# Hybrid decoder layer on one core: a square moved ahead, two pipeline points one step later, and a weight load inside a DRAM exchange

## The reference

```
p = rms_norm(h_res, norm_mix_g) @ w_in
xc, b_gate, c_gate = split(p[..., :3072], 3)
y_conv = b_gate * conv3(c_gate * xc, conv_w)
z = p + (prev_token(p) - p) * mu          # token shift of r, k, v and the low-rank parts
kk = k * k_k ; kk = kk / max(norm_per_head(kk), 1e-12)
S_t = S_{t-1} * w_t + (S_{t-1} @ a_t) b_t^T + v_t k_t^T ;  y_t = S_t @ r_t
y = layer_norm_per_head(y) * lnx_w + lnx_b + sum(r * k * r_k) * v ;  y = y * g
h_res += concat(y_conv, y) @ w_out
h_res += relu(rms_norm(h_res) @ w_up)^2 @ w_down ;  out = rms_norm(h_res)
```

## Time and profile before

| | |
|---|---|
| median of 3 runs | 2480.15 us (2478.11 to 2480.57) |
| the profiled execution's own time | 2474.11 us |
| its span | 2472.4 us |
| PE busy | 2421.4 us (98%) |
| DVE busy | 1128.8 us (46%) |
| ACT busy | 784.8 us (32%) |
| the eight pairs | about 112 to 868 us of the span |

### The profile page before, as it was taken

One profiled execution on the slowest core, in us unless ns is written; L12 is line 12 of the kernel. 1 busy time (PEld: TensorE's weight loads), 2 busy tenths in 40 slices (PEclk: granted clock), 3 DMA queues, 4 the chain that ended last, 5 costly groups with the idle time before them and its releaser, 6 DMA issues.

```text
span 2472.4 us, 41991 instructions
## 1 busy us (share of the span) xinstructions
PE 2421.4 (98%) x16510; PEld 2046.5 (83%) x16510; DVE 1128.8 (46%) x1725; ACT 784.8 (32%) x1320; POOL 184.8 (7%) x224
## 2 busy tenths in 40 slices
PE   6999999999999999999999999999999999999997
PEld 6989989989989778788888888888888888888886
DVE  6367567576576654533333333333233333333343
ACT  6434343334334322332232232222222221322233
POOL 4001001011010132000000000000000000000032
PEclk8999999999999999999999999999999999999999
DMA  8333343342442643323233333233233333332332
GB/s 209 90 91 79 94 97 80 87 101 73 97 97 78 176 138 90 89 86 108 81 107 98 86 102 94 84 104 94 86 104 94 93 101 87 87 110 81 98 94 94
DMA packets 506892, 243.65 MB, mean 99 GB/s; under 512 B 102992, under 2 KB 500688, under 8 KB 506192
## 3 DMA queue, kind: packets, MB, share of 16 engines
q1 hardware_dynamic: 500512, 222.70, 33.3%
q0 software_dynamic: 6208, 18.37, 2.3%
HBM read 224.08 MB, written 16.92 MB: 97 GB/s over the span
## 4 chain that ended last, share of the span: by engine, by line
PE 88%; DVE 4%; DMA 4%; ACT 2%; issue 1%; SPq 1%; ACTq 0%; DVEq 0%
PE PD L1349 64%; PE PD L1352 17%; PE PD L1540 1%; DMA w_raw<-in_w_in 1%; DMA gram<-NA 1%; DMA inverse<-UU 1%; DVE w_lo L948 1%; DMA UU<-gram 1%; PE PW L1503 1%; DMA x_rows<-in_x 0%; DVE act_lo L953 0%; PE PW L1405 0%; DVE uni L1112 0%; PE PW L1467 0%; PE PW L1382 0%
## 5 line engine op out<-in xcount | busy, mean ns | idle before, releaser
L948 DVE TENSOR_TENSOR w_lo<-w_raw,w_hi 128x512 fp32r<-128x512 f32 x780 | 543.9, 731 | 308.2 <-ACT w_hi L684 305.0
L684 ACT CAST w_hi<-w_raw 128x512 fp32r<-128x512 f32 x780 | 456.7, 620 | 705.8 <-PE PD L1349 518.4
L1349 PE MATMUL PD<-act_lo,w_hi 128*128 128x512 f32 x1344 | 531.3, 395 | 0.0
L1349 PE MATMUL PD<-act_hi,w_hi 128*128 128x512 f32 x1344 | 529.2, 394 | 1.5 <-DVE res L1225 1.5
L1349 PE MATMUL PD<-act_hi,w_lo 128*128 128x512 f32 x1344 | 528.5, 393 | 0.0
L1349 PE MATMUL PD<-u_hi,w_hi 128*128 128x512 f32 x1024 | 409.7, 400 | 0.0
L1349 PE MATMUL PD<-u_hi,w_lo 128*128 128x512 f32 x1024 | 403.4, 394 | 0.0
L1349 PE MATMUL PD<-u_lo,w_hi 128*128 128x512 f32 x1024 | 401.5, 392 | 0.0
L1352 PE MATMUL PD<-act_hi,w_hi 128*128 128x264 f32 x1376 | 297.9, 298 | 10.0 <-DVE act_lo L953 9.9
L1349 PEld LDWEIGHTS PD<-act_hi,w_hi 128*128 128x128 f32 x1344 | 252.5, 188 | 63.4 <-DVE w_lo L948 1.9
L1349 PEld LDWEIGHTS PD<-act_lo,w_hi 128*128 128x128 f32 x1344 | 252.0, 188 | 58.2 <-issue 0.2
(11 more groups left out here) (278 smaller groups left out, 1571.8 us busy)
## 6 DMA issues: line engine op xcount, KB each, us to landing
w_raw<-in_w_up SPq DMA_DIRECT2D x256, 256.0 KB, 3.3
w_raw<-in_w_down SPq DMA_DIRECT2D x256, 256.0 KB, 3.1
w_raw<-in_w_in SPq DMA_DIRECT2D x200, 256.0 KB, 3.3
w_raw<-in_w_out SPq DMA_DIRECT2D x64, 256.0 KB, 2.8
x_rows<-in_x SPq DMA_DIRECT2D x4, 1024.0 KB, 8.0
residual<-res POOLq DMA_DIRECT2D x2, 2048.0 KB, 11.9
out<-rows SPq DMA_DIRECT2D x8, 512.0 KB, 4.9
uni<-inverse SPq DMA_DIRECT2D x16, 240.0 KB, 4.2
```

The source lines that it names most:

```text
L684: nc.scalar.copy(w_hi[:, q % RING], w_raw[:, q % RAW]).then_inc(hi_split, 1)
L948: V.tensor_tensor(w_lo[:, q % RING], w_raw[:, q % RAW], w_hi[:, q % RING].bitcast(F32), ALU.subtract).then_inc(lo_split, 1)
L1349: ins = M(pd_seq(n), w, v[:, k, first:first + SEQ], start=begin, stop=end)
```

## The change

The table changes five numbers: `tr` and `amv` each get one dense step more ahead of them, `ahead4` and `ahead5` one less. Running sums before: tr 28, gram1, base1 and base2 31, amv 33, ahead3 45, ahead4 50, ahead5 54. After: tr 29, gram1, base1 and base2 32, amv 35, ahead3 47, ahead4 51, ahead5 54. From x16 on nothing in the table moves. The square of the keys of pair j+1 is issued by ScalarE in the last name of pair j, ahead of the copies of the value tile, with a semaphore of its own. The read half of the second exchange moves from load 17 to load 18.

```diff
@@ -68,13 +68,13 @@
 
 
 
-PACE = dict(ss=2, low=5, vtr=5, ahead0=6, gram0=8, tr=2, gram1=3, base1=0, base2=0, amv=2, ahead1=4, ahead2=4,
-            ahead3=4, ahead4=5, ahead5=4, x16=3, t16=2, x32=2, tt32=2, pq=2, gh=3, y0=5, z2=4, z3=2, z4=1, z5=2, z6=1,
+PACE = dict(ss=2, low=5, vtr=5, ahead0=6, gram0=8, tr=3, gram1=3, base1=0, base2=0, amv=3, ahead1=4, ahead2=4,
+            ahead3=4, ahead4=4, ahead5=3, x16=3, t16=2, x32=2, tt32=2, pq=2, gh=3, y0=5, z2=4, z3=2, z4=1, z5=2, z6=1,
             z7=2, z8=2, y=2, var=3, ahead6=4)
 
 PE_STEPS = [n for n in PACE if n[:4] != "base" and n[:5] != "ahead"]
 Z_STEPS = ("z2", "z3", "z4", "z5", "z6", "z7", "z8")
-ACT_STEPS = ["sq", "nrm", "for_sig", "sigw", "siga", "for_exp", "vtok", "epv", "em", "ep", "gs", "ghi", "btok",
+ACT_STEPS = ["nrm", "for_sig", "sigw", "siga", "for_exp", "vtok", "epv", "em", "ep", "gs", "ghi", "btok",
              "ktok", "bonb", "atok", "mv", "t16", "tt32", "warm", "pq", "sqc", "yk", "std"]
 DVE_STEPS = (["kk", "ssm", "inv", "ld", "scan", "mid", "mu", "epv", "gs", "kkn", "tfac", "kp",
               "at", "b", "bt", "rt", "kt", "rb", "gram0", "bon", "glo", "gram1", "diag"]
@@ -317,7 +317,7 @@
     low_done, low_sig, low_top = sem("low_done"), sem("low_sig"), sem("low_top")
     gram_out, gram_back = sem("gram_out"), sem("gram_back")
     inv_out, inv_back, inv_cleared = sem("inv_out"), sem("inv_back"), sem("inv_cleared")
-    z_done = sem("z_done")
+    z_done, k_squared = sem("z_done"), sem("k_squared")
     conv_step = sem("conv_step")
     conv_stored, y_stored = sem("conv_stored"), sem("y_stored")
     zeroed = sem("zeroed")
@@ -443,6 +443,7 @@
                 dve("ut")
                 for m in range(2):
                     sp.dma_start(inv_blocks[:, m], UU[0:NBLK, 1 - m, :].rearrange("b (s t) -> b s t", t=BASE)).then_inc(inv_out, 16)
+            if i == 18:
                 sp.wait_ge(inv_out, at(32, 32, j))
                 for a in range(2):
                     r = slice(a * C, (a + 1) * C)
@@ -708,6 +709,10 @@
             nc.scalar.copy(halves(shifted[0:rows_, 1:T + 1]), pd(n)[0:rows_])
             nc.scalar.activation(halves(keep[0:rows_, :]), pd(n)[0:rows_], ACT.Copy, scale=mun).then_inc(evacuated[n % 2], 1)
 
+        def square_keys(j):
+            act.wait_ge(z_done, at(5, 3, j))
+            nc.scalar.activation(fsq, zk[:], ACT.Square, scale=p_("k_k", j)).then_inc(k_squared, 1)
+
 
         act.wait_ge(zeroed, 2)
         act.wait_ge(par_loaded, N_PAR)
@@ -718,6 +723,8 @@
             if n == 5:
                 for q in range(Q_PAIR + EDGE_LEAD, Q_PAIR + LEAD):
                     split(q)
+            if n == 5:
+                square_keys(0)
             take_shifted(n, 4 * (n + 1), mun[0:rows_], z_before=n if n else None, rows_=rows_)
             for q in range(4 * n + 8, 4 * n + 12):
                 if q < Q_PAIR + EDGE_LEAD:
@@ -762,7 +769,6 @@
 
             def steps_of(name):
                 if name == "ss":
-                    done("sq", nc.scalar.activation(fsq, zk[:], ACT.Square, scale=feat("k_k")))
                     dve("ssm")
                     done("nrm", nc.scalar.activation(fsq, fsq, ACT.Sqrt))
                     done("for_sig", nc.scalar.activation(warm[:], eps_t[:, 0:1], ACT.Sigmoid))
@@ -813,6 +819,8 @@
                 if name == "var":
                     pe("var")
                     done("std", nc.scalar.activation(ysq, PW[:, 0, :], ACT.Sqrt, bias=eps_t[:, 1:2]))
+                if name == "ahead6" and not last:
+                    square_keys(j + 1)
 
             splits, tiles, y_split = 0, 0, 0
             for name, k in zip(PACE, schedule()):
@@ -1377,7 +1385,7 @@
 
             def steps_of(name):
                 if name == "ss":
-                    act("sq")
+                    pe.wait_ge(k_squared, j + 1)
                     for a in range(2):
                         ins = M(PW[:, 2 + a, 0:HALF], same_head[:], half(fsq, a), start=True, stop=True)
                 if name == "low":
```

## The result

The changed kernel takes 2487.96 us (median of 6 runs, 2486.32 to 2490.15), the kernel before on the same chip 2478.0 us (2474.04 to 2480.57). The ratio is 1.004, 95% interval 1.0027 to 1.0053: slower by about 10 us, which is more than the measurement's uncertainty. The forecast was 2493.7 us, in a range of 2476 to 2506. Against the profiled executions' own times (2474.11 and 2487.06 us) the change costs 12.95 us; the sum said 13.6. The profiled execution of the kernel before is one of its quickest, 3.9 us under the median of the six, and the changed kernel's lies 0.9 us under its own.

The account below looks back on a forecast made before the run. The prediction took TensorE's own matmuls as the bound, with about 12 us of waits. Its terms, -5.4 + 16.8 - 1.0 + 3.2 = +13.6 us, gave 2487.7 us, plus 6.0 to the median: 2493.7 us, range 2476 to 2506.

Parts of the forecast that it names:

- the sum: Whole kernel: -5.4 + 16.8 - 1.0 + 3.2 = +13.6 us against the profiled execution's 2474.1 us.
- The inversion is later: On VectorE: inversion starts 4.00 us later (0.60 + 3.40), less earlier DMA waits of 3.5 us over the pairs.
- A new wait at x16: TensorE at x16, first seven pairs: waits 1.5 to 2.5 us for the reads of the inverted blocks.
- t16: TensorE at t16: 2.80 us later in pairs 0 to 4, 2.23 in 5 and 6; +16.8 us together.
- The square: At the start of each pair: TensorE's wait for the square goes in all eight, -5.4 us, between 0 and 6.
- Contention of the gate's store: The store of `cx` falls beside the reads and load 18: 0.45 us in seven pairs, +3.2 us.
- The clock: Rival: clock falls to half level behind new waits in seven pairs, +11.9 us, 2505.6 us; chance 0.12.
- The last pair: Inversion only 2.2 us later, t16 0.2 us earlier, part of L1540's 1.8 us wait goes: -1.0 us.
- The late landing of the write: Second exchange: write up to 1.8 us later per pair, unsummed; as rival +6.4 us, 2500.1 us, chance 0.08.
- load 18 landed: Rival: load 18 quicker by 2 us or more, so x16 alone sets t16; 2479 us, no change; chance 0.15.
- "faster" rival: Way from `ut` to x16 has over 4 us of slack, all waits go: -13.4 us, 2466.8 us; chance 0.15.

Follow-up runs that it names:

- e1: The changed kernel with VectorE's split of quarter 13 and the convolution put back behind the inversion: 2457.99 us, ratio 0.9925 to the kernel before.
- e5: The kernel before with only the new numbers of the table, square and load 17 as before: 2502.76 us, ratio 1.0113.
- e6: The kernel before with quarter 13's split and the convolution ahead of the inversion on VectorE, quarter 13's rounding ahead of ScalarE's AMV copies: 2501.06 us, ratio 1.0096.
- e2: The kernel before with only the square of the keys issued ahead of the value tile's copies: 2468.93 us, ratio 0.997.
- e3: The kernel before with only load 17 moved between the write and the reads of the second exchange: 2469.67 us, ratio 0.9973.
- e9: The changed kernel with the table of before, so only the square ahead and load 17 between write and reads: 2460.35 us, ratio 0.9927 to the kernel before.
- e10: e1 run once more on the same chip as e9: 2459.52 us, ratio 0.9928 to the kernel before.
- e4: The kernel before with only VectorE's split of quarter 13 and the convolution put ahead of the inversion: 2531.38 us, ratio 1.0223.
- e7: The kernel before with the new numbers of the table and the convolution held behind the inversion: 2479.76 us, ratio 1.0013.

## Why the prediction was right

The direction and the mechanism held: five VectorE instructions ahead of the inversion, a chain through DRAM that passes the delay on, and a new wait at x16. The forecast of +13.6 us stands against 12.9 between the traces and 10.0 between the medians. The forecast time of 2493.7 us is 5.7 us too high: 3.6 us by the sum, and 2.1 since the three runs of before that it started from have a median 2.15 us over that of the six. Its range held the result. Point by point, in times of the two traces:

- **The inversion is later.** Forecast 4.00 us less the DMA waits it had before, which is 26.3 us over pairs 0 to 6; the table of starts gives 24.9. The block was right (3.41 us against 3.40). The shift of tr was put at 0.60 us and came to less: tr starts 0.50 us later after gram0 (3.54 in place of 3.04), and `KA` 0.40 us (9.24 in place of 334.43 - 325.59 = 8.84). e1, e5 and e6 show that this delay is the cause.
- **A new wait at x16.** Forecast 1.5 to 2.5 us in seven pairs. It was 2.1 to 3.8 us, and in the last pair too (2.69 us), where I had none. About 0.5 us of each wait costs nothing, since TensorE comes to x16 that much sooner after gram0 (28.44 in six of the eight pairs of e1, where it doesn't wait, against 28.95 before). The slack of 2.5 us was read in pair 2 with a median landing of 4.1 us; by the landings in the trace it was 1.9 to 2.2 us in pairs 2 to 6, 0.8 in pair 0 and 0.2 in pair 1. Two pairs stand out after the change. In pair 0 the reads were issued 4.92 us behind the write. In pair 7 they took longer to land: from the last read's issue to x16 it was 6.3 us, against 4.20 us in pair 2 (353.77 to 357.97).
- **t16.** Forecast +16.8 us over pairs 0 to 6, measured 3.49 + 1.74 + 2.82 + 2.35 + 2.30 + 3.00 + 2.98 = 18.7 us, clock included. In pairs 1 and 4 TensorE ran at half clock between x16 and t16, and t16 came 0.81 and 0.74 us after it could have (L1139's start + 0.74). Without that it is 17.1 us. The total agrees better than its parts: the forecast was 2.80 us in each of pairs 0 to 4 and 2.23 in 5 and 6, and only pair 2 has what was forecast. Pairs 1, 3 and 4 lost less, pairs 0, 5 and 6 more, and that this cancels is luck.
- **The square.** Forecast -5.4 us, measured more. Gram0 of pair 0 came 2.74 us sooner (135.44, 132.70), and each following boundary gave 0.7 us where the clock did not fall: 2.74 + 7 x 0.7 = 7.6 us, and e2 measured 7 to 8 us by itself. Of the 2.74 us, 0.4 lie ahead of the square: L1382 in pair 0 starts at 111.70 in place of 114.37, and only 2.3 us of that are the gap in front of it. So about 7.2 us are the square's. The term was mis-sized: I took the wait by the modelled end of the matmul before (0.47 us) as a price. The gap by starts is 304.53 - 303.89 = 0.64 us, and from L1382 to gram0 it takes 0.08 us less too. The 6 us that the prediction gave as the most was too low as well.
- **Contention of the gate's store.** Forecast +3.2 us, between 0 and 6.4. It is there, but not where TensorE waits. The gate's store took longer to land, 4.8 us in the median against 3.6 before (5.9 in e3, 6.0 in e9), and only GpSimd waits for it, once, 3.7 us in place of 2.2. Load 18 landed 4.7 to 5.4 us behind its issue; load 17 took 5.5 to 5.9 us before in pairs 0 to 4 and 4.4 in pairs 5 and 6. The four reads took SyncE 0.4 us longer to issue in pair 2 (351.39 to 354.49 against 345.94 to 348.67). From the end of `ut` to the landing of the last read it was 70.8 us over pairs 0 to 6, against 70.5 before.
- **The clock.** It had 0.12 as a rival with seven falls of 1.7 us, and nothing in the sum. There were five, and the one that the kernel before has in its last pair was gone. Their cost was not 1.7 us each, since part of each fell into time in which TensorE waited anyway: 0.81 + 0.74 at t16 in pairs 1 and 4, and 0.63, 0.74 and 0.78 us between t16 and the next gram0 in pairs 0, 3 and 6 (over 61.99), together 3.7 us.
- **The last pair.** Forecast -1.0 us, measured -0.4, by another way. The prediction had no wait at x16 here and the fall of the clock behind L1540 as before. But the wait at L1540 (now L1548) was 1.0 us and not 1.8, and no fall followed it, so TensorE stood at x16 about 2.4 us sooner (32.50 - 2.69 = 29.81 against 32.25 us after gram0). There it waited for the reads and lost nearly all of it. That the two numbers are near each other is luck.

By these terms: -7.6 + 17.1 + 3.7 - 0.4 = 12.8 us of 12.9. All four are differences of starts, so that they add up proves no cause; the causes rest on the experiments. The sum of 13.6 came out well partly because a gain of the square that was put too low (by 2.2 us, of which 0.4 are not the square's) and a contention that TensorE did not meet (3.2 us) stood against a clock cost that I had left out (3.7 us).

The late landing of the write was left out of the sum, and rightly: the reads were issued 3.24 us behind the write with load 17 between in seven pairs, and 4.92 us behind it in pair 0. The long way in that one pair does not need load 17: e5, which has no load there, shows 4.69 us in its pair 0. The Trainium skill, "DMA: Bandwidth & Descriptors", section "Latency and other measured facts", says that a DMA's fixed cost grows with the load on the memory; no run here shows that one load behind the write does it.

The rivals: load 18 landed at most 1.1 us sooner than load 17 had, not 2 or more; the way from `ut` to x16 had no 4 us of slack. The "faster" rival named rightly what the other two parts remove, but its 13.4 us for all waits gone was too low: e9 and e10 measured 19 us.

What stays open is why the clock falls in one pair and not in the next. The waits at x16 were 3.77, 2.12, 2.18, 2.71, 2.30, 2.67, 2.43 and 2.69 us. It fell behind the 2.12 and not behind the 2.18, 2.67 and 2.69. So the length of the wait alone does not decide in this range. I made no run for it.

## What to carry to other kernels

A table that paces several engines at once sets what else falls beside each name, not only when the name comes. Before moving an entry by one, list what each engine does at the sums that are crossed (here 32), and read the order of instructions on the engine that feeds the longest chain. A chain through DRAM (VectorE, write, landing, reads) with some 2 us of slack deserves the head of every queue it passes; work that only fills time goes behind its start. A load may go into such a chain's waiting time if its own condition is met by then: load 17 was worth 7 us, load 18 cost 15, since it held the queue for a split that was not done.

## What the runs showed of the hardware

- With two DMAs more beside the exchange (load 17 right behind the write, the gate's store beside the reads) the reads were issued 3.24 us behind the write in seven pairs, as before. What got slower is the gate's store: 4.8 us from issue to landing in the median against 3.6, and 6.0 in e9.
- The write's way can be longer with nothing queued behind it: 4.69 us to the first read in pair 0 of e5, and 3.66 to 4.82 us in pairs 2 to 6 of e4. Why isn't shown.
- The granted clock fell to its half level behind some waits of 2.1 to 3.8 us and not behind others of the same length. In e4, where the waits at x16 came to 40.1 us, up to 6.6 us each, it fell in every pair.
- A fall of 3.4 us cost 0.6 to 0.8 us where its first part lay in time in which TensorE would have waited for VectorE. In pair 5 of e7, where it lay behind t16 and nothing waited, it cost 1.5 us (64.22 in place of 62.7 us from t16 to the next gram0).
